# Who issues the loads of activations and gates in the value stage of a product-key expert layer

## Chip, cores and metric

The kernel runs on one core of one Trainium2 chip. The metric is the device time of one execution in microseconds, as the median of several runs. One more execution is taken under the hardware profiler, and every row of the trace below is from it.

## What is computed

One layer of a streaming encoder for 544 frames (512 of a prompt and 32 of a running stream) of width 1024, in float32: token mixers of two convolution groups, then a product-key retrieval over 128 x 128 experts with one neuron each, 8 heads with 16 experts per frame. Only the second half of the retrieval matters here:

```
act = gelu(einsum('td,thkd->thk', xt, u))      # u: the chosen experts' input rows
out = einsum('thk,thkd->td', gate * act, v)    # v: their output rows
```

For 384 of the 544 frames ("dense") the kernel doesn't gather. It multiplies them with all 16384 experts and lets a gate that is zero for the experts not chosen do the choosing. For the last 160 frames it gathers the chosen rows one slot at a time.

## The kernel before

The work goes through a stream of 300 units of weights, each 128 x 1024 float32 (512 KB): 20 of the input projection, 8 of the output projection, 16 of queries, 128 of u and 128 of v. A ring of four buffers (`raw`) takes them in. For near-float32 products, each unit is split in two: ScalarE copies it to `w_hi` (line 967), and GpSimd (line 504) or, from the value stage on, VectorE (line 1614) makes the rest `w_lo`. TensorE then runs three products for each chunk of 128 columns: hi x hi, hi x lo and lo x hi. A weight buffer is loaded again as soon as its unit is split (`load`, line 408, on the sync engine SP).

The u stage leaves the activations of each unit in DRAM (`acts_dram`, in pairs, line 1130) and the gates too (`gates_dram`, twelve groups of 32 frames, line 1175); both stores are issued by ScalarE. The value stage reads them back. A *quarter* is the activations of four units (768 KB, line 420) and goes to one of two buffers `acts_in`. A *group* is the gates of 16 units; it goes to `gates_even` or `gates_odd` in three pieces of 1 MB (line 426).

In the value stage VectorE's order for v = 0 to 127 is: the product of activations and gates of unit v + 4 (line 1651); one or two gathered rows added to the sums (line 1468); `w_lo` of unit v + 2 (line 1614); and `prod_lo` of unit v + 3 (line 1660). ScalarE's order is: `w_hi` of unit v + 2 (line 967), then `prod_hi` of unit v + 3 (line 1184), which waits for its product and until TensorE has finished unit v - 1, since `prod_hi` has four buffers. TensorE takes the units in order (line 912): 8 chunks, three products each. GpSimd fetches the gathered rows (line 568), up to eight ahead.

SP's order in this stage is written out in `value_group` (line 457). For each quarter it waits until the quarter's four products are made, issues the load of the quarter after next, then one piece of the next group's gates (quarters 0 to 2 of a group), then four loads of weights, each of which waits for the `w_lo` of the unit that had the buffer. So one queue carries weights, activations and gates. The loads of group 0's gates and of quarters 0 and 1 are issued ahead of the stage (lines 445 to 448).

Of the kernel before, what the change touches and what calls it, by code (L numbers as in the profile page):

```python
# [51 lines left out]
RING = 4  # L52
N_IN, N_OUT, N_Q = 5 * WC, KC, 2 * HEADS
N_U = NKEYS
N_V = NKEYS
GROUP = 16
GROUPS = N_V // GROUP
QUARTER = 4
QUARTERS = GROUP // QUARTER
GATE_PIECES = 3  # L60
# [20 lines left out]
GTS = DENSE // GT  # L81
# [17 lines left out]
AHEAD = 3  # L99
# [41 lines left out]
def build(nc, stream, x_t, params, sub_keys, u_rows, v_rows, final_g, y_t, y_rows, caches):  # L141
    gates_dram = nc.dram_tensor("gates_dram", (GTS, P, NKEYS, GT), F32, kind="Internal").ap()
    acts_dram = nc.dram_tensor("acts_dram", (N_U // 2, P, 2 * DENSE), F32, kind="Internal").ap()

    with ExitStack() as ctx:
        def sb_in(stack, name, shape, dt=F32):
            return stack.enter_context(nc.sbuf_tensor(name, shape, dt))
# [4 lines left out]
        def sem(name):  # L152
            return ctx.enter_context(nc.semaphore(name))
# [95 lines left out]
        acts_in = sb_in(values, "acts_in", [P, 2, QUARTER // 2, 2 * DENSE])  # L249
# [4 lines left out]
        gates_in = (gates_even, gates_odd)  # L254
# [56 lines left out]
        act_saved = [sem(f"act_saved{s}") for s in range(2)]  # L311
        acts_back = [sem(f"acts_back{s}") for s in range(2)]
        gates_back = [sem(f"gates_back{s}") for s in range(2)]
        prod_made = sem("prod_made")
# [63 lines left out]
        def wait_split(engine, lap, j, by_dve):  # L378

            if by_dve:  # L380
                engine.wait_ge(low_made, RING * (lap - LOW_LAP) + j + 1)
            else:
                engine.wait_ge(hi_made, RING * lap + j + 1)
                engine.wait_ge(lo_made, RING * lap + j + 1)
# [18 lines left out]

        @block.sync
        def _(sp):
            def load(lap, j, by_dve=False):

                if not (isinstance(lap, int) and lap == 0):  # L410
                    wait_split(sp, lap - 1, j, by_dve)
                src = stream[bass.ds(RING * lap + j, 1)].rearrange("a p n -> p (a n)")
                sp.dma_start(raw[:, j, :], src).then_inc(raw_in[j], 16)

            def load_acts(quarter, s):

                for n in range(2):
                    sp.wait_ge(act_saved[n], 16 * (quarter + 1))
                acts = acts_dram[bass.ds(2 * quarter, 2)].rearrange("e p t -> p e t")
                sp.dma_start(acts_in[:, s], acts).then_inc(acts_back[s], 16)  # L420

            def load_gates(group, s, piece):

                part = slice(piece * GTS // GATE_PIECES, (piece + 1) * GTS // GATE_PIECES)
                g = gates_dram[part, :, bass.ds(GROUP * group, GROUP), :].rearrange("g p e t -> p g (e t)")
                sp.dma_start(gates_in[s][:, part].rearrange("p g e t -> p g (e t)"), g).then_inc(gates_back[s], 16)

            def load_x(k):
                sp.dma_start(hid[:, k], x_t[:, k]).then_inc(x_in[k], 16)

            load_x(0)
            load(0, 0)
            for k in range(1, KC):
                load_x(k)
            for j in range(1, RING):
                load(0, j)
            first_load = FIRST_V // RING - U_AFTER + 2
            with sp.Fori(1, first_load) as lap:
                for j in range(RING):
                    load(lap, j)  # L440

            sp.wait_ge(g_saved[0], 16 * ((GTS + 1) // 2))
            sp.wait_ge(g_saved[1], 16 * (GTS // 2))
            first_value = FIRST_V // RING
            for piece in range(GATE_PIECES):
                load_gates(0, 0, piece)
            for s in range(2):
                load_acts(s, s)
            for lap in range(first_load, first_value + 1):
                for j in range(RING):  # L450
                    load(lap, j)
            for j in range(2):
                load(first_value + 1, j, True)
            sp.wait_ge(act_took, N_IN + N_Q + N_U)
            sp.dma_start(gain_rows[:], final_g).then_inc(gain_in, 16)

            def value_group(pair_lap, s, quarters=QUARTERS, gates_too=True):

                group = 2 * pair_lap + s
                for q in range(quarters):  # L460
                    sp.wait_ge(prod_made, GROUP * group + QUARTER * (q + 1))
                    load_acts(QUARTERS * group + q + 2, q % 2)
                    if q < GATE_PIECES and gates_too:
                        load_gates(group + 1, 1 - s, q)
                    for j in range(2, RING):
                        load(first_value + QUARTERS * group + q + 1, j, True)
                    for j in range(2):
                        load(first_value + QUARTERS * group + q + 2, j, True)

            with sp.Fori(0, GROUPS // 2 - 1) as pair_lap:  # L470
                value_group(pair_lap, 0)
                value_group(pair_lap, 1)
            value_group(GROUPS // 2 - 1, 0)
            value_group(GROUPS // 2 - 1, 1, QUARTERS - 2, gates_too=False)
            for j in range(2, RING):
                load(N_UNITS // RING - 1, j, True)
            sp.wait_ge(row_used, 2 * SLOTS)
            for g in range(PARTS):
                sp.dma_start(rows[0:PACKED, g, :], sums_x[g * PACKED:(g + 1) * PACKED, :]).then_inc(parts_in, 16)
            sp.wait_ge(y_rows_made, 1)  # L480
            sp.dma_start(y_rows[0:P], y_rows_sb[:]).then_inc(y_rows_saved, 16)
            sp.wait_ge(y_rows_made, 2)
            sp.dma_start(y_rows[P:GATHERED], rows[0:PACKED, PARTS, :]).then_inc(y_rows_saved, 16)
            sp.wait_ge(y_rows_saved, 32)
            sp.wait_ge(y_saved, 16 * 2 * len(Y_PIECES))
            sp.wait_ge(cache_saved, 16)
# [473 lines left out]
        def _(act):  # L960
            def split_high(lap, j):

                lap, j = lap + j // RING, j % RING
                act.wait_ge(raw_in[j], 16 * (lap + 1))
                if not (isinstance(lap, int) and lap == 0):
                    act.wait_ge(unit_done, RING * (lap - 1) + j + 1)
                nc.scalar.activation(w_hi[:, j, :], raw[:, j, :], ACT.Copy).then_inc(hi_made, 1)  # L967
# [49 lines left out]
            for u in range(N_IN):  # L1017
                c, part = (u - 2 * WC) // 3, (u - 2 * WC) % 3
# [161 lines left out]
            def product_high(v):  # L1180
                act.wait_ge(prod_made, v + 1)
                if v >= RING:
                    act.wait_ge(unit_done, FIRST_V + v - RING + 1)
                nc.scalar.activation(prod_hi[:, v % RING], prod[:, v % 2], ACT.Copy).then_inc(prod_hi_made, 1)  # L1184
# [18 lines left out]
            for v in range(N_V):  # L1203
                if v < N_V - 2:
                    split_high(FIRST_V // RING, v + 2)
                if v < N_V - AHEAD:
                    product_high(v + AHEAD)
                if v == 0:
                    act.wait_ge(row_used, SLOTS)
                    nc.scalar.activation(gelu[:], dots[:], ACT.Gelu).then_inc(gelu_made, 1)  # L1210
                if v == LAST_SUM + 2:
                    act.wait_ge(row_sum_made, 1)
                    nc.scalar.activation(row_std[:, 0:1], row_sum[:, 0:1], ACT.Sqrt, bias=eps[:],
                                         scale=1.0 / D).then_inc(row_std_made, 1)
                if v == LAST_SUM + 5:
                    act.wait_ge(row_sum_made, 2)
                    nc.scalar.activation(row_std[0:PACKED, 1:2], row_sum[0:PACKED, 1:2], ACT.Sqrt, bias=eps[0:PACKED],
                                         scale=1.0 / D).then_inc(row_std_made, 1)
# [602 lines left out]
```

## Time and profile before

| | us |
|---|---|
| runs shown | 1496.18, 1498.42, 1496.32 |
| median | 1496.32 |
| the profiled execution | 1497.36 |
| its span, from first to last instruction | 1495.5 |
| TensorE busy | 1444.0 |
| VectorE busy | 1249.6 |
| ScalarE busy | 630.6 |

The profiled execution is 1.86 us longer than its span, and 1.04 us above the median of the runs. The value stage lasts from about 937 us to the last matmuls near 1478 us. Busy times count instructions that compute; issuing a DMA and waiting don't count.

### The profile page before, as it was taken

What the parts mean: (1) busy time and instruction counts of PE and PEld (TensorE: products, weight loads), DVE (VectorE), ACT (ScalarE), POOL (GpSimd) and SP (SyncE); (2) the same over time, 40 slices, a digit from 0 to 9 for tenths busy, and PEclk for the clock granted to TensorE, in tenths of its full rate; (3) what the DMA queues carried; (4) which work ended last, traced back from release to release, by engine and by line L of the source; (5) the groups of instructions that cost most, each with busy time, mean ns of one, the idle gap of its engine ahead of it and who ended that gap; (6) DMA issues with size and microseconds to landing.
All of it is one profiled execution on the core that took longest, in us unless ns stands there. A gap on an engine that the chain in (4) does not pass through costs nothing.

```text
span 1495.5 us, 26608 instructions
## 1 busy us (share of the span) xinstructions
PE 1444.0 (97%) x9308; PEld 1423.0 (95%) x9308; DVE 1249.6 (84%) x2536; ACT 630.6 (42%) x848; POOL 886.8 (59%) x558
## 2 busy tenths in 40 slices
PE   7998989999999999999999997999999999999995
PEld 7998989999999999999999997999999999999984
DVE  7999874798999988688878841899999999999985
ACT  6234543333333333466666652333333333333331
POOL 4687434557688888666766675355555555555401
PEclk9999999999999999999999999999999999999997
DMA  4222213648699999789999999999999999999931
GB/s 179 97 77 69 98 59 120 218 171 296 211 339 330 323 344 335 257 325 352 379 359 364 367 370 329 388 378 396 386 409 380 410 386 375 407 380 414 357 115 46
DMA packets 125988, 433.37 MB, mean 290 GB/s; under 512 B 12480, under 2 KB 14784, under 8 KB 124256
## 3 DMA queue, kind: packets, MB, share of 16 engines
q1 hardware_dynamic: 66256, 211.57, 39.5%
q0 software_dynamic: 46080, 167.79, 29.6%
q10 hardware_dynamic: 13584, 53.25, 9.0%
q8 instruction: 24, 0.39, 0.1%
q14 instruction: 44, 0.36, 0.1%
HBM read 379.35 MB, written 52.69 MB: 289 GB/s over the span
## 4 chain that ended last, share of the span: by engine, by line
PE 81%; DVE 1%; DMA 1%; issue 0%; POOL 0%; ACT 0%; DVEq 0%; ACTq 0%
PE ps_unit L842 35%; PE ps_unit L912 18%; PE ps_misc L912 18%; PE ps_unit L817 6%; PE ps_misc L877 3%; DMA raw<-stream 1%; PE ps_misc L782 1%; PE ps_misc L786 0%; DVE y_sb L1760 0%; PE ps_unit L769 0%; DVE rows L1714 0%; DVE gate_parts L1603 0%; DVE gate L1556 0%; DVE rstd L1757 0%; POOL w_lo L504 0%
## 5 line engine op out<-in xcount | busy, mean ns | idle before, releaser
L504 POOL TENSOR_TENSOR w_lo<-raw,w_hi 128x1024 fp32r<-128x1024 f32 x172 | 415.8, 2419 | 215.4 <-issue 134.1
L568 POOL DMA_INDIRECT rows<-v_rows,expert x160 | 256.9, 1606 | 232.8 <-DVE sums L1468 159.9
L842 PE MATMUL ps_unit<-mov_hi,w_hi 128*128 128x384 f32 x1024 | 352.3, 344 | 8.6 <-POOL w_lo L504 8.6
L842 PE MATMUL ps_unit<-mov_lo,w_hi 128*128 128x384 f32 x1024 | 346.0, 338 | 0.0
L842 PE MATMUL ps_unit<-mov_hi,w_lo 128*128 128x384 f32 x1024 | 345.0, 337 | 0.0
L967 ACT ACTIVATE w_hi<-raw 128x1024 fp32r<-128x1024 f32 x300 | 315.2, 1051 | 60.2 <-ACT act_ring L1140 33.2
L1458 DVE CUSTOM_DVE_ANT_0 rows<-rows,ps_unit 128x1024 f32<-128x1024 f32 x160 | 190.4, 1215 | 30.1 <-DMA rows<-u_rows,expert 30.0
L1184 ACT ACTIVATE prod_hi<-prod 128x384 fp32r<-128x384 f32 x128 | 67.4, 526 | 320.8 <-PE ps_misc L912 320.4
L842 PEld LDWEIGHTS ps_unit<-mov_hi,w_hi 128*128 128x128 f32 x1024 | 193.1, 189 | 9.1 <-issue 9.1
L842 PEld LDWEIGHTS ps_unit<-mov_lo,w_hi 128*128 128x128 f32 x1024 | 193.3, 189 | 0.0
L842 PEld LDWEIGHTS ps_unit<-mov_hi,w_lo 128*128 128x128 f32 x1024 | 192.8, 188 | 0.0
L912 PE MATMUL ps_unit<-prod_hi,w_hi 128*128 128x384 f32 (+1 forms) x520 | 174.6, 336 | 6.2 <-DVE w_lo L1614 5.6
L912 PE MATMUL ps_unit<-prod_lo,w_hi 128*128 128x384 f32 (+1 forms) x520 | 174.1, 335 | 0.0
L912 PE MATMUL ps_unit<-prod_hi,w_lo 128*128 128x384 f32 (+1 forms) x520 | 173.9, 334 | 0.0
L568 POOL DMA_INDIRECT rows<-u_rows,expert x160 | 152.9, 955 | 33.8 <-issue 19.1
L1140 ACT ACTIVATE act_ring<-ps_unit 128x384 f32<-128x384 f32 x128 | 62.8, 491 | 257.1 <-PE ps_unit L842 257.1
L912 PE MATMUL ps_misc<-prod_hi,w_lo 128*128 128x384 f32 x508 | 169.9, 335 | 0.0
L912 PE MATMUL ps_misc<-prod_lo,w_hi 128*128 128x384 f32 x508 | 169.9, 334 | 0.0
L912 PE MATMUL ps_misc<-prod_hi,w_hi 128*128 128x384 f32 x508 | 169.8, 334 | 0.0
L1468 DVE SCALAR_TENSOR_TENSOR sums<-rows,weight,sums 128x1024 f32<-128x1024 f32 x128 | 163.8, 1280 | 3.6
L1614 DVE TENSOR_TENSOR w_lo<-raw,w_hi 128x1024 fp32r<-128x1024 f32 x128 | 155.9, 1219 | 4.2 <-issue 2.6
L1660 DVE TENSOR_TENSOR prod_lo<-prod,prod_hi 128x384 fp32r<-128x384 f32 x128 | 71.2, 556 | 47.6 <-ACT prod_hi L1184 46.5
(255 smaller groups left out, 2773.4 us busy)
## 6 DMA issues: line engine op xcount, KB each, us to landing
raw<-stream SPq DMA_DIRECT2D x300, 512.0 KB, 6.0
acts_dram<-act_ring ACTq DMA_DIRECT2D x64, 384.0 KB, 6.8
gates_dram<-gates ACTq DMA_DIRECT2D x12, 2048.0 KB, 10.8
acts_in<-acts_dram SPq DMA_DIRECT2D x32, 768.0 KB, 8.9
gates_even<-gates_dram SPq DMA_DIRECT2D x12, 1024.0 KB, 13.6
gates_odd<-gates_dram SPq DMA_DIRECT2D x12, 1024.0 KB, 12.9
rows<-u_rows,expert POOLq DMA_INDIRECT x160, 6.6
rows<-v_rows,expert POOLq DMA_INDIRECT x160, 8.1
```

The lines of the kernel that those rows point to most:

```text
L504: nc.gpsimd.tensor_tensor(w_lo[:, j, :], raw[:, j, :], w_hi[:, j, :].bitcast(F32), ALU.subtract).then_inc(lo_made, 1)
L568: nc.gpsimd.indirect_dma_start(out=rows[:, n % ROWS_RING, :], out_offset=None, in_=table, in_offset=bass.IndirectOffsetOnAxis(ap=expert[:, ...
L817: last = nc.tensor.matmul(ps_unit[:, a, 0:HALF], w[:, u % RING, k * P:(k + 1) * P], half(mov[:, k], a), start=(k == 0 and m == 0), stop=(k ...
L842: last = nc.tensor.matmul(dense_psum(j), w[:, j, k * P:(k + 1) * P], m[:, k, 0:DENSE], start=(k == 0 and n == 0), stop=(k == KC - 1 and n ...
L912: ins = nc.tensor.matmul(out, w[:, j, k * P:(k + 1) * P], m[:, j, part], start=(first and n == 0), stop=(last and n == 2))
L967: nc.scalar.activation(w_hi[:, j, :], raw[:, j, :], ACT.Copy).then_inc(hi_made, 1)
L1140: nc.scalar.activation(act_ring[:, j], dense_psum(j), ACT.Gelu).then_inc(act_took, 1)
L1184: nc.scalar.activation(prod_hi[:, v % RING], prod[:, v % 2], ACT.Copy).then_inc(prod_hi_made, 1)
L1458: nc.vector.tensor_tensor_reduce(out=rows[:, n % ROWS_RING, :], in0=rows[:, n % ROWS_RING, :], in1=x_rows, scale=1.0, scalar=0.0, op0=ALU. ...
L1468: nc.vector.scalar_tensor_tensor(out=total[:], in0=rows[:, n % ROWS_RING, :], scalar=weight[:, s:s + 1], in1=total[:], op0=ALU.mult, op1=A ...
L1614: nc.vector.tensor_tensor(w_lo[:, j, :], raw[:, j, :], w_hi[:, j, :].bitcast(F32), ALU.subtract).then_inc(low_made, 1)
L1660: nc.vector.tensor_tensor(prod_lo[:, v % RING], prod[:, v % 2], prod_hi[:, v % RING].bitcast(F32), ALU.subtract).then_inc(prod_lo_made, 1)
```

## The change

The two functions that load activations and gates take the issuing engine as an argument. SP still issues group 0's gates and quarters 0 and 1. All others are issued by ScalarE, in its loop over v: behind `prod_hi` of the last unit of a quarter (v + 3 = 3, 7, 11, ...) it issues the activations of the quarter after next and, for the first three quarters of a group, a piece of the next group's gates. SP's loop keeps four loads of weights per lap and has no wait for products.

```diff
+        def load_acts(engine, quarter, s):
+            for n in range(2):
+                engine.wait_ge(act_saved[n], 16 * (quarter + 1))
+            acts = acts_dram[bass.ds(2 * quarter, 2)].rearrange("e p t -> p e t")
+            engine.dma_start(acts_in[:, s], acts).then_inc(acts_back[s], 16)
+        def load_gates(engine, group, s, piece):
...
-                load_gates(0, 0, piece)
+                load_gates(sp, 0, 0, piece)
...
-                load_acts(s, s)
+                load_acts(sp, s, s)
...
-            def value_group(pair_lap, s, quarters=QUARTERS, gates_too=True):
-                group = 2 * pair_lap + s
-                for q in range(quarters):
-                    sp.wait_ge(prod_made, GROUP * group + QUARTER * (q + 1))
-                    load_acts(QUARTERS * group + q + 2, q % 2)
-                    if q < GATE_PIECES and gates_too:
-                        load_gates(group + 1, 1 - s, q)
-                    for j in range(2, RING):
-                        load(first_value + QUARTERS * group + q + 1, j, True)
-                    for j in range(2):
-                        load(first_value + QUARTERS * group + q + 2, j, True)
...
+            def value_lap(lap):
+                for j in range(2, RING):
+                    load(first_value + lap + 1, j, True)
+                for j in range(2):
+                    load(first_value + lap + 2, j, True)
+            with sp.Fori(0, N_V // RING - 2) as lap:
+                value_lap(lap)
...
                 if v < N_V - AHEAD:
                     product_high(v + AHEAD)
+                    quarter = (v + AHEAD) // QUARTER
+                    if (v + AHEAD) % QUARTER == QUARTER - 1 and quarter + 2 < N_V // QUARTER:
+                        load_acts(act, quarter + 2, quarter % 2)
+                        group, piece = quarter // QUARTERS, quarter % QUARTERS
+                        if piece < GATE_PIECES and group + 1 < GROUPS:
+                            load_gates(act, group + 1, (group + 1) % 2, piece)
```

## Rows read from the trace of the kernel before

**Rows 1.** Page, part 1: busy us (share of the span), instructions.

```profile
PE 1444.0 (97%) x9308; PEld 1423.0 (95%) x9308; DVE 1249.6 (84%) x2536; ACT 630.6 (42%) x848; POOL 886.8 (59%) x558
```

**Rows 2.** Stretches: length, busy of each engine, granted clock, DMA share, GB/s.

```profile
1045.00:1095.00 50.00, 50.00 (x290) 50.00 (x289) 46.12 (x53) 17.95 (x24) 25.67 (x17) 1.00 1.00 392
1145.00:1195.00 50.00, 50.00 (x290) 50.00 (x289) 46.70 (x53) 17.72 (x24) 27.03 (x17) 1.00 1.02 410
```

**Rows 3.** Chain that ended last, 945 to 1440 us, by line.

```profile
by line: PE ps_misc L912 50.1%; PE ps_unit L912 50.0%
```

**Rows 4.** Waits, 945 to 1440 us: total us, times, longest.

```profile
ACT prod_hi L1184 <- PE ps_misc L912: 309.8, 118, 3.0
...
DVE prod_lo L1660 <- ACT prod_hi L1184: 23.4, 35, 1.4
...
ACT w_hi L967 <- DMA raw<-stream: 8.8, 6, 2.5
```

**Rows 5.** Waits, 850 to 1490 us: those of PE.

```profile
PE ps_unit L842 <- POOL w_lo L504: 8.6, 1, 8.6
...
PE ps_unit L912 <- DVE w_lo L1614: 5.6, 1, 5.6
```

**Rows 6.** ScalarE in order of time, 700 to 730 us: start, length, instruction, idle before.

```profile
707.02 0.49 ACT L1140 ACTIVATE act_ring<-ps_unit 128x384 f32<-128x384 f32 x1 [1.73 <-PE ps_unit L842]
707.54 0.34 ACTq L1130 DMA_DIRECT2D acts_dram<-act_ring  x1
707.92 0.45 ACTq L1175 DMA_DIRECT2D gates_dram<-gates  x1
708.47 1.06 ACT L967 ACTIVATE w_hi<-raw 128x1024 fp32r<-128x1024 f32 x1 [0.96 <-ACT act_ring L1140]
...
718.40 1.06 ACT L967 ACTIVATE w_hi<-raw 128x1024 fp32r<-128x1024 f32 x1 [0.47 <-ACT act_ring L1140]
```

**Rows 7.** ScalarE in order of time, 1165 to 1200 us.

```profile
1170.32 0.53 ACT L1184 ACTIVATE prod_hi<-prod 128x384 fp32r<-128x384 f32 x1 [2.68 <-PE ps_misc L912]
...
1182.80 0.53 ACT L1184 ACTIVATE prod_hi<-prod 128x384 fp32r<-128x384 f32 x1 [2.68 <-PE ps_misc L912]
...
1195.28 0.53 ACT L1184 ACTIVATE prod_hi<-prod 128x384 fp32r<-128x384 f32 x1 [2.68 <-PE ps_misc L912]
```

**Rows 8.** Tile acts_in, SP, 883 to 900 us: issue ns min/median/max; us to landing.

```profile
L420 SPq DMA_DIRECT2D acts_in<-acts_dram x2: 3400/4208/5016, 888.5 to 893.6; - x2
...
DMA to landing us min/median/max: 19.3/20.9/22.4
```

**Rows 9.** SP's queue in order of time, 1150 to 1204 us.

```profile
1167.57 0.38 SPq L420 DMA_DIRECT2D acts_in<-acts_dram  x1
1168.14 0.38 SPq L426 DMA_DIRECT2D gates_even<-gates_dram  x1
```

**Rows 10.** VectorE in order of time, 1180 to 1200 us.

```profile
1183.36 0.56 DVE L1660 TENSOR_TENSOR prod_lo<-prod,prod_hi 128x384 fp32r<-128x384 f32 x1 [0.68 <-ACT prod_hi L1184]
1184.05 0.56 DVE L1651 TENSOR_TENSOR prod<-acts_in,gates_even 128x384 f32<-128x384 f32 x1
...
1187.11 1.22 DVE L1614 TENSOR_TENSOR w_lo<-raw,w_hi 128x1024 fp32r<-128x1024 f32 x1
```

**Rows 11.** Tile gates_even, SP, 945 to 1440 us.

```profile
DMA to landing us min/median/max: 12.2/13.2/15.6
```

**Rows 12.** Tile gates_even, SP, 883 to 890 us.

```profile
DMA to landing us min/median/max: 12.8/17.2/19.8
```

**Rows 13.** VectorE's groups, 945 to 1440 us: busy us, mean ns, idle before.

```profile
L1468 DVE SCALAR_TENSOR_TENSOR sums<-rows,weight,sums 128x1024 f32<-128x1024 f32 x128 | 163.8, 1280 | 3.6
...
L1468 DVE SCALAR_TENSOR_TENSOR sums_x<-rows,weight,sums_x 128x1024 f32<-128x1024 f32 x32 | 40.9, 1280 | 0.8
```

**Rows 14.** Tile acts_in, SP, 945 to 1440 us.

```profile
DMA to landing us min/median/max: 4.9/8.8/11.4
```

**Rows 15.** DMA queues, 945 to 1440 us: packets, MB, share of 16 engines.

```profile
q1 hardware_dynamic: 36394, 108.26, 56.3%
```

More of the change, by code:

```diff
@@ L401, in out_psum @@
             return sum_psum(q - 2) if q in (2, 3) else unit_psum(q)
+        def load_acts(engine, quarter, s):
[4 more added lines that the diff above has]
+        def load_gates(engine, group, s, piece):
+            part = slice(piece * GTS // GATE_PIECES, (piece + 1) * GTS // GATE_PIECES)
+            g = gates_dram[part, :, bass.ds(GROUP * group, GROUP), :].rearrange("g p e t -> p g (e t)")
+            engine.dma_start(gates_in[s][:, part].rearrange("p g e t -> p g (e t)"), g).then_inc(gates_back[s], 16)
         @block.sync
@@ L413, in load @@
                 sp.dma_start(raw[:, j, :], src).then_inc(raw_in[j], 16)
[L415 to L426, printed above, removed]
             def load_x(k):
@@ L455, in _ @@
             sp.dma_start(gain_rows[:], final_g).then_inc(gain_in, 16)
-            def value_group(pair_lap, s, quarters=QUARTERS, gates_too=True):
-                group = 2 * pair_lap + s
-                for q in range(quarters):
-                    sp.wait_ge(prod_made, GROUP * group + QUARTER * (q + 1))
-                    load_acts(QUARTERS * group + q + 2, q % 2)
-                    if q < GATE_PIECES and gates_too:
-                        load_gates(group + 1, 1 - s, q)
-                    for j in range(2, RING):
-                        load(first_value + QUARTERS * group + q + 1, j, True)
-                    for j in range(2):
-                        load(first_value + QUARTERS * group + q + 2, j, True)
[L470 to L474, printed above, removed]
+            def value_lap(lap):
[5 more added lines that the diff above has]
+                value_lap(lap)
             for j in range(2, RING):
```

## The prediction

> **What bounds the kernel now.** I read the page's first part, then the stretches of the value stage, then its chain and its waits, then single instructions around one group border. The page shows TensorE (PE) busy for 97% of the span, VectorE (DVE) for 84% and ScalarE (ACT) for 42% [rows 1]. The change touches only the value stage, so shares of the span settle nothing. In two stretches of that stage PE is busy 50.00 of 50.00 us at full granted clock, ACT about 18, DVE about 46.5, and the DMA share is at 1.0 while 392 to 410 GB/s move [rows 2]. The chain from 945 to 1440 us consists of PE's value matmuls and nothing else [rows 3]. The waits of that stretch name ACT (309.8 us waiting for PE before prod_hi), DVE (23.4 us waiting for ACT's prod_hi) and ACT once more (8.8 us for raw weights), but never PE [rows 4]. PE's waits lie at the stage's two ends: 8.6 us as the last u units starve, and 5.6 us near 1455 us, when DVE adds the packed rows before the last w_lo [rows 5]. So PE sets the time here, and anything the change does must reach PE to count.
>
> **The change part by part.** It moves 51 issues: the loads of quarters 2 to 31 (30 activation loads) and the gates of groups 1 to 7 in three pieces each (21). It takes SP's wait on prod_made out, and makes SP's loop one lap of four weight loads.
>
> *Weights no longer behind activations and gates: 0 us.* What earlier weights could shorten is a wait for raw. In this stretch only ACT has one, 8.8 us in six places [rows 4], on an engine with 309.8 us to spare, and DVE and PE never wait for w_hi there. The five loads that open the stage stay on SP, so the jam behind PE's 8.6 us stays [rows 5]. The 5.6 us stay too: they hang on DVE's order.
>
> *ACT's time for the issues: 0 us on the path.* ACT already issues such DMAs in the u stage: with one issue the gap to its next activation is 0.47 us, with two 0.96 [rows 6]. 21 pairs and 9 single ones make 21 x 0.96 + 9 x 0.47 = 24 us, beside 309.8 us idle. One at a time: an issue stands before the next w_hi, and ACT has 2.68 us free before each prod_hi [rows 7]. The new waits on act_saved are for spills long landed. What is queued behind the issue is w_hi, then prod_hi; DVE waits for them, and PE for DVE. The bad end is an issue that blocks: when five loads were issued in a row on SP, the activation issues took up to 5.0 us [rows 8]. That would make prod_hi 5.0 - 2.7 = 2.3 us late, under the cover worked out below. I take 0.96, since one pair at a time is the row that is alike.
>
> *The issue's place: this is where something gets late.* Near 1168 us SP issues the activations at 1167.57 and the gates at 1168.14 [rows 9]. The gates are the third piece of an even group. Their first reader is the DVE product at 1184.05, the first from gates_even, v = 64 [rows 10]. It follows, in order, the prod_lo of v = 62 at 1183.36, for which ACT's prod_hi started at 1182.80; three back, the prod_hi of v = 59 starts at 1170.32 [rows 7, 10]. Behind that one the change puts the issue. With the offsets of the u stage (first issue 0.52 us after the activation's start, second 0.38 later [rows 6]) the activations go out at 1170.84 and the gates at 1171.22: 3.1 us later than now. The gates may then take 1184.05 - 1171.22 = 12.8 us without anybody waiting.
>
> How long they will take on ACT's queue no row shows. The nearest row is the landing on SP's queue, 12.2 to 15.6 us with 13.2 in the middle [rows 11]; the far one is the pile of five loads at 884 us, 12.8 to 19.8 [rows 12]. I place it by what is left over. Weights need 524 kB per 4.16 us unit (three units from prod_hi at 1182.80 to that at 1195.28 [rows 7]), 126 GB/s. Gathered rows need 160 x 524 kB in 117 units, 172 GB/s (160 adds [rows 13], between FIRST_SUM 3 and LAST_SUM 120). Of 410 GB/s [rows 2] that leaves 112, and activations and gates of one quarter, 1.84 MB, take 16.4 us, the gates 16 from their own issue. I take 16 and keep 12.2 and 19.8 as ends. DVE then waits 16 - 12.8 = 3.2 us at a group border.
>
> For this one term a page speaks against the change. On one queue the trace shows 13.2 us in the middle [rows 11]. The Trainium skill (DMA: Bandwidth & Descriptors, section Queues, rings and completion order) says that each DMA engine goes round the queues that have work, one packet a turn. Here the code's runs are 4 KB for weights and rows, 3 KB for activations and 2 KB for gates. One run a packet is near what is counted, 36394 packets for 108.26 MB or 3.0 kB each on SP's queue [rows 15]. If all three queues are always full, activations get 3/11 and gates 2/10 of 410 GB/s, and both are in after 7.0 + 12.8 = 19.8 us, so that DVE would wait some 6.5 us; no run here shows it yet.
>
> *What hides DVE's wait.* In the iteration that starts with this product, DVE goes on to w_lo of v = 62, over at 1187.11 + 1.22 = 1188.33 [rows 10]. PE begins unit 62 when unit 61 is done, and that releases the prod_hi at 1195.28 [rows 7]: 6.95 us of cover. 3.2 us fit in it. DVE makes the delay good: its 23.4 us of waits for prod_hi [rows 4] over 495 / 4.16 = 119 units are 0.2 us a unit, 3 us a group. A DVE that runs late also needs the next gates later, so the wait doesn't add up from group to group. Activations alone are safe: 13.2 us from issue to the same product, against 11.4 at most [rows 14].
>
> *Sum.* 0 on PE from each part. The profiled execution took 1497.36 us for a span of 1495.5, 1.04 above the median of 1496.32; 0 added to that median is **1496.3 us**.
>
> **The rivals.** **Gates too late for PE (slower).** Place: the product that opens each of groups 1 to 7. From 12.8 + 6.95 = 19.8 us of landing on, the cover is gone and PE stops by what is beyond, each time anew, since PE's own delay moves ACT's issue as well. At 20.5 us that is 7 x 0.7 = 5 us (1501); at 22.4, the longest landing of the pile, the activations' [rows 8], 7 x 2.6 = 18 us (1514). For it speaks that the DMA engines are full [rows 2] and that 112 GB/s is only just over the 1.84 MB per 16.6 us quarter (110 GB/s) that the queue must carry. Against it: once DVE waits, weights and rows ask for less, and the gates get the rest. The packet turns of the page above would put the landing right at this point; the trace as it stands neither bears that out nor excludes it.
>
> **Earlier weights help after all (faster).** Its bound is PE's last wait, 5.6 us [rows 5], which would need an earlier last w_lo: 1490.7 at best. Against it: that w_lo stands behind DVE's row sums, not behind a transfer.
>
> **ACT's queue blocks at each pair.** At 5.0 us an issue [rows 8] DVE would get prod_hi 2.3 us late on top of 3.2 us for gates, 5.5 in all, still under 6.95: 1496.3. It only adds to the first rival's chance.
>
> **How the numbers follow.** A measurement of this kernel tells some 0.2% (3 us) from no change; the runs shown lie within 1496.18 to 1498.42. The forecast (PE never stops for it) gets 0.72, the late gates 0.23, the gain 0.04, the rest 0.01. A loss by late gates under 3 us would count as the same, one above as slower: 0.23 for slower, 0.04 for faster, 0.73 for the same. The range goes from 1493.8, the forecast less most of the 3 us, to 1504, which takes in the late gates up to about 1 us per group; the forecast's own range is 1494 to 1499.3.
>
> **What the changed profile would show.** Right: no wait of PE between 945 and 1440 us; acts_in and gates issues under ACTq about 3 us later than SP's; a new wait of DVE at line 1651 for gates, some seven times and 1 to 4 us each, with the 23.4 us of waits for prod_hi falling by about as much; raw landing sooner than before; ACT's gap before w_hi near 1 us every fourth unit. Wrong: PE waits for w_lo or prod_lo inside that stretch (the first rival), gates landing beyond 19.8 us, or activations that hold DVE in the middle of a group.

## The result, and the profile after

The changed kernel takes 1507.65 us (median of 4 runs, 1506.70 to 1511.19). The kernel before, run beside it, takes 1497.37 us (1496.18 to 1498.92). The ratio is 1.0071, with a 95% interval of 1.0054 to 1.0088: **slower by 0.7%**, some 10 us. The profiled execution took 1506.70 us for a span of 1504.9, so its span is 9.4 us longer than that of before.

The stretches of the value stage (columns as in [rows 2]) show where PE is no longer full:

```profile
1150.00:1184.00 34.00, 34.00 (x198) 34.00 (x197) 33.27 (x38) 13.14 (x17) 18.91 (x13) 1.00 1.03 414
...
1186.00:1197.00 11.00, 9.05 (x53) 8.73 (x51) 4.29 (x5) 3.06 (x4) 2.07 (x2) 1.00 0.69 278
1197.00:1204.00 7.00, 7.00 (x31) 7.00 (x32) 6.83 (x9) 2.42 (x4) 4.04 (x3) 0.76 0.90 291
```

Up to 1184 us all is as before: PE full, DMA engines full. In the eleven microseconds from 1186 us DVE is busy for 4.29 only and PE loses 2. Then PE is busy again, but with a granted clock of 0.76. The waits of 945 to 1450 us (total, times, longest) name what stood still:

```profile
ACT prod_hi L1175 <- DVE prod L1648: 36.7, 10, 5.2
ACT w_hi L958 <- DMA raw<-stream: 24.4, 24, 2.4
DVE prod L1648 <- DMA gates_odd<-gates_dram: 18.5, 4, 7.7
DVE prod L1648 <- DMA gates_even<-gates_dram: 18.3, 3, 7.9
...
ACT w_hi L958 <- issue: 8.4, 14, 0.8
...
DVE prod_lo L1657 <- ACT prod_hi L1175: 6.2, 9, 1.4
...
PE ps_unit L903 <- DVE w_lo L1611: 5.9, 5, 2.0
```

Against [rows 4], DVE has two new rows: it waits seven times for gates, once per group, 36.8 us in all. Its wait for prod_hi has shrunk from 23.4 to 6.2 us, and PE has a row where it had none: 5 waits for w_lo, 5.9 us. One border of groups, the same as in [rows 7, 9, 10], shows the chain in order. First ScalarE (start, length, instruction, idle before):

```profile
1170.12 0.53 ACT L1175 ACTIVATE prod_hi<-prod 128x384 fp32r<-128x384 f32 x1 [2.68 <-PE ps_misc L903]
1170.20 0.37 ACTq L411 DMA_DIRECT2D acts_in<-acts_dram  x1
1170.60 0.50 ACTq L417 DMA_DIRECT2D gates_even<-gates_dram  x1
1171.20 1.06 ACT L958 ACTIVATE w_hi<-raw 128x1024 fp32r<-128x1024 f32 x1 [0.55 <-issue]
```

Then VectorE:

```profile
1184.16 0.55 DVE L1657 TENSOR_TENSOR prod_lo<-prod,prod_hi 128x384 fp32r<-128x384 f32 x1
1192.60 0.56 DVE L1648 TENSOR_TENSOR prod<-acts_in,gates_even 128x384 f32<-128x384 f32 x1 [7.89 <-DMA gates_even<-gates_dram]
...
1195.66 1.22 DVE L1611 TENSOR_TENSOR w_lo<-raw,w_hi 128x1024 fp32r<-128x1024 f32 x1
```

And the chain of waits over 1150 to 1210 us (start, length, what), which before held nothing but PE [rows 3]:

```profile
1170.60 21.93 DMA gates_even<-gates_dram
...
1192.60 0.06 DVE prod L1648
...
1195.66 1.23 DVE w_lo L1611
...
1196.94 3.81 PE ps_unit L903 x12
1200.74 2.21 PE ps_misc L903 x12
```

The gates are issued at 1170.60, 2.5 us later than before, and land at 1192.5 instead of 1180.3. DVE needed them at about 1184.7, stands for 7.89 us, makes w_lo at 1195.66 instead of 1187.11, and PE, which wanted it at 1195.0, begins at 1196.94. Its first twelve matmuls then take 3.81 us instead of 2.08.

Over the stage, the landing of gates by tile (gates_even, then gates_odd, 945 to 1440 us) answers to [rows 11]:

```profile
DMA to landing us min/median/max: 16.9/20.2/21.9
...
DMA to landing us min/median/max: 12.0/18.7/22.3
```

From a median of 13.2 us the landing of gates_even has gone to 20.2. Weights land in 7.3 us (median) as before; activations went from 8.8 to 9.1, gathered rows from 8.1 to 9.4.

Of the 9.4 us in the span, 5.9 are PE's waits, and 1.9 the slow matmuls behind the first of them (3.81 + 2.21 instead of 2 x 2.08). Behind three of the four other stops the first twelve matmuls take 2.35 to 2.37 us at a granted clock of 1.00, 0.8 us more together than at 2.08. The rest, under 1 us, is not accounted for.

### The profile page after: what moved, and what is told of

Read it like the earlier page. It is cut to its first block, busy times and chain, and to the rows that moved or that the text cites. A ratio compares the mean times of both kernels' runs of the same rounds, so it can differ in the third digit from the quotient of the medians.

```text
span 1504.9 us, 26602 instructions
## 1 busy us (share of the span) xinstructions
PE 1446.2 (96%) x9308; PEld 1423.3 (95%) x9308; DVE 1244.6 (83%) x2536; ACT 635.7 (42%) x848; POOL 888.0 (59%) x558
## 4 chain that ended last, share of the span: by engine, by line
PE 74%; DMA 7%; DVE 2%; issue 1%; ACT 0%; POOL 0%; ACTq 0%; DVEq 0%
PE ps_unit L833 35%; PE ps_unit L903 15%; PE ps_misc L903 14%; PE ps_unit L808 6%; PE ps_misc L868 3%; DMA gates_odd<-gates_dram 3%; DMA gates_even<-gates_dram 3%; DMA raw<-stream 1%; PE ps_misc L773 1%; DVE w_lo L1611 0%; DVE sums L1465 0%; PE ps_misc L777 0%; DVE y_sb L1757 0%; PE ps_unit L760 0%; DVE rows L1711 0%
## 5 line engine op out<-in xcount | busy, mean ns | idle before, releaser
L903 PE MATMUL ps_unit<-prod_hi,w_hi 128*128 128x384 f32 (+1 forms) x520 | 175.9, 338 | 12.1 <-DVE w_lo L1611 11.5
L903 PEld LDWEIGHTS ps_unit<-prod_hi,w_hi 128*128 128x128 f32 x520 | 98.9, 190 | 14.3 <-DVE w_lo L1611 13.4
## 6 DMA issues: line engine op xcount, KB each, us to landing
gates_even<-gates_dram ACTq DMA_DIRECT2D x9, 1024.0 KB, 20.2
```

The lines of the kernel that those rows point to most:

```text
L903: ins = nc.tensor.matmul(out, w[:, j, k * P:(k + 1) * P], m[:, j, part], start=(first and n == 0), stop=(last and n == 2))
```

## Experiments

The theory is **sharing**: the gates land late because activations and gates, on a queue of their own, get only that queue's turns at the DMA engines. The rivals are **place** (the issue is 2.5 to 3 us later, and that alone does it) and **ScalarE's own work** (51 more issues on it). All ratios are against the kernel before, run on the same chip.

**1. Late issue, old queue.** The kernel before, with SP held back to where ScalarE issues:

```diff
-                    sp.wait_ge(prod_made, GROUP * group + QUARTER * (q + 1))
+                    sp.wait_ge(prod_hi_made, GROUP * group + QUARTER * (q + 1))
```

> The kernel before, with one edit: SP waits for the prod_hi of a quarter's last unit instead of its products, so that it issues activations and gates where ScalarE does after the change, some 3 us later, but still on the one queue with the weights. Theory (sharing: a queue of its own gets only a share of the DMA engines' turns): the third gates still land in 12 to 15.6 us, DVE waits at most 3 us at a group border, PE never stops between 945 and 1440 us, and the time is that of the kernel before within 0.2%. Rival (place: the 3 us later issue alone does it): DVE waits 5 to 8 us at the borders, PE stops in the stage, and the time is near 1507 us.

Measured: 1497.02 us, ratio 0.9997 (0.9987 to 1.0006). The landing of gates_even, then DVE's one wait for it:

```profile
DMA to landing us min/median/max: 10.0/11.0/14.3
...
DVE prod L1651 <- DMA gates_even<-gates_dram: 2.2, 1, 2.2
```

The gates even land a little sooner than the 12 to 15.6 us expected, and PE never waits between 945 and 1440 us. On the old queue, place alone costs nothing.

**2. Early issue, new queue.** The changed kernel, ScalarE issuing one unit sooner:

```diff
-                    if (v + AHEAD) % QUARTER == QUARTER - 1 and quarter + 2 < N_V // QUARTER:
+                    early = (v + AHEAD) % QUARTER == QUARTER - 2
+                    if (early or v == 0) and quarter + 2 < N_V // QUARTER:
+                        act.wait_ge(prod_made, QUARTER * (quarter + 1))
                         load_acts(act, quarter + 2, quarter % 2)
```

> The changed kernel, with ScalarE's issues one unit (4.16 us) earlier, behind the prod_hi of the last unit but one of a quarter and a wait for the quarter's last product; only the first quarter's stays. Three queues as after the change. Sharing: the third gates still take 19 to 22 us to land, DVE's wait at a border falls from up to 7.9 us to at most 4, which is under the cover of 6.95 us, so PE doesn't stop and the time is back within 0.2% of before. Place alone: gates land in about 13 us and DVE waits nowhere. Rival (ScalarE's own work: the issues delay w_hi and prod_hi): as many issues, so the loss of some 10 us stays.

Measured: 1498.46 us, ratio 1.0003 (0.9994 to 1.0013). Gates_even and gates_odd land thus, and PE is full from 945 to 1395 us:

```profile
DMA to landing us min/median/max: 13.2/15.5/20.7
...
DMA to landing us min/median/max: 15.1/17.9/20.8
...
945.00:1395.00 450.00, 450.00 (x2598) 450.00 (x2597) 416.12 (x470) 163.25 (x218) 239.49 (x146) 1.00 1.00 391
```

The transfers are still slow, if less so than expected (third gates 13 to 20 us, not 19 to 22), but no longer late: DVE's longest wait for gates is 2.8 us. ScalarE has as many issues as after the change, so its own work is out.

**3 and 4. One of the two kinds of load back on SP.**

Both restore SP's `value_group` with its wait for products. In run 3 SP issues the gates there, and ScalarE's `load_gates` goes:

```diff
+                    sp.wait_ge(prod_made, GROUP * group + QUARTER * (q + 1))
+                    if q < GATE_PIECES and gates_too:
+                        load_gates(sp, group + 1, 1 - s, q)
...
-                            load_gates(act, group + 1, (group + 1) % 2, piece)
```

> The changed kernel with the gates back on SP at their place of before (SP's loop written out); ScalarE issues only the activations. Sharing: the gates have the weights' queue and nothing of the activations ahead of them, so they land in about 12 us or less, DVE doesn't wait for gates, PE doesn't stop, and the time is within 0.2% of before; the activations land in 8 to 12 us, in time. Rival (any third queue slows all of them): gates over 16 us, DVE waits, PE stops, time over 1502 us.

In run 4 it is the other way round:

```diff
+                    sp.wait_ge(prod_made, GROUP * group + QUARTER * (q + 1))
+                    load_acts(sp, QUARTERS * group + q + 2, q % 2)
...
-                        load_acts(act, quarter + 2, quarter % 2)
```

> The changed kernel with the activations back on SP at their place of before; ScalarE issues only the gates, 3 us later than before. Sharing, with the queue's length as the reason: 1 MB alone on ScalarE's queue lands in 10 to 15 us, DVE waits at most 2 us at a border, PE doesn't stop, time within 0.2% of before. If the gates' 2 KB runs against 4 KB ones set their share, whatever lies ahead: 1.05 MB at 82 GB/s, 13 to 16 us, DVE waits up to 3 us, PE still doesn't stop. Rival (place alone): DVE waits as after the change and the time stays near 1507 us.

Measured: with the gates on SP 1497.65 us, ratio 1.0000 (0.9990 to 1.0009); with the activations on SP 1497.49, ratio 0.9997 (0.9988 to 1.0007). In the first the gates land in 12.6 us (median, 15.2 at most), a little above the 12 expected, and DVE never waits for them. In the second the gates are alone on ScalarE's queue and land thus (gates_odd), while DVE waits for them five times, 11.5 us in all, and PE never:

```profile
DMA to landing us min/median/max: 12.9/15.4/17.5
```

That is nearer the second of the two expectations, in which the 2 KB runs set the gates' share whatever lies ahead of them; DVE's longest wait, 4.0 us, is beyond its 3. So the loss needs both loads on the one new queue, the gates behind the activations. Place alone is out a second time: here the gates are issued as late as after the change.

**5. The dose raised.** The changed kernel, issuing one unit later:

```diff
-                    quarter = (v + AHEAD) // QUARTER
-                    if (v + AHEAD) % QUARTER == QUARTER - 1 and quarter + 2 < N_V // QUARTER:
+                    quarter = (v + AHEAD) // QUARTER - 1
+                    if v > 0 and (v + AHEAD) % QUARTER == 0 and quarter + 2 < N_V // QUARTER:
```

> The changed kernel, with ScalarE's issues one unit (4.16 us) later, the dose raised. The gates may now take 12.8 - 4.2 = 8.7 us before DVE waits and 8.7 + 6.95 = 15.6 before PE stops. Sharing with a deadline: at landings of 19 to 21 us PE stops 3 to 5 us at each of seven borders, 21 to 35 us in all, so 1518 to 1533 us. Rival (the loss is what ScalarE spends on issues, or the third queue slows transfers everywhere): as many issues and queues as after the change, so the time stays near 1507 us.

Measured: 1533.0 us, ratio 1.0231 (1.0214 to 1.0248). The waits from 945 to 1480 us, and two stretches around one border:

```profile
DVE prod L1648 <- DMA gates_odd<-gates_dram: 34.3, 4, 9.8
DVE prod L1648 <- DMA gates_even<-gates_dram: 29.7, 3, 10.5
...
PE ps_unit L903 <- DVE w_lo L1611: 22.3, 6, 4.8
```

```profile
1120.00:1137.00 17.00, 14.35 (x83) 14.03 (x81) 7.27 (x9) 3.67 (x6) 5.05 (x4) 1.00 0.78 311
1137.00:1150.00 13.00, 11.37 (x56) 11.37 (x57) 12.79 (x15) 4.93 (x7) 7.31 (x5) 0.87 0.83 295
```

PE stops at six of the seven borders (at the first the gates land in 14.8 us), 3.7 us each, within the 3 to 5 expected. The median is at the upper end of the forecast, because the waits are not the whole price: behind this stop the granted clock is 0.87 over 13 us. Behind each of the six, 24 matmuls take 6.0 to 7.1 us instead of 4.16, some 13 us in all, and with the 22.3 us of waits that makes up the loss of 34.9.

**6. The weights' runs halved: told nothing.**

```diff
...
+                if by_dve:
+                    src = src.rearrange("a p (h n) -> p (a h) n", h=2)
+                    sp.dma_start(raw[:, j, :].rearrange("p (h n) -> p h n", h=2), src).then_inc(raw_in[j], 16)
...
```

> The changed kernel, with each value weight load asked for in runs of 2 KB where it had 4 KB; same bytes, same places. If the DMA engines take turns packet by packet and a run is a packet, weights now get 2 KB per turn, the gates' share rises from 2/10 to 2/8, and activations and gates are in after about 16 us: the third gates land in 15 to 18 us, PE stops little or not at all, the time falls to 1497 to 1502 us, and raw takes longer to land than 7.3 us. Rival (shares go by bytes, or by what each queue asks): gates still land in 19 to 22 us, time near 1507 us.

Measured: 1505.24 us, ratio 1.0047 (1.0031 to 1.0064). The weights' queue (packets, MB, share), after the change and in this run:

```profile
q1 hardware_dynamic: 16760, 60.99, 31.4%
```

```profile
q1 hardware_dynamic: 16856, 61.38, 31.7%
```

Half-size runs would have added 128 packets to each of 116 loads. They didn't: the bytes per packet are the same, and the run is in effect a repeat of the changed kernel.

**7. The gates' runs doubled.** The changed kernel with another layout of the gates in DRAM, so that a load finds 4 KB in one piece:

```diff
-    gates_dram = nc.dram_tensor("gates_dram", (GTS, P, NKEYS, GT), F32, kind="Internal").ap()
+    gates_dram = nc.dram_tensor("gates_dram", (GTS // 2, P, GROUPS, 2, GROUP * GT), F32, kind="Internal").ap()
...
+            g = gates_dram[part.start // 2:part.stop // 2, :, group].rearrange("g p b n -> p g (b n)")
+            dst = gates_in[s][:, part].rearrange("p (g b) e t -> p g (b e t)", b=2)
...
+                act.dma_start(gates_dram[tg // 2, :, :, tg % 2, :],
+                              gates[:, s].rearrange("p (g e) t -> p g (e t)", e=GROUP)).then_inc(g_saved[s], 16)
```

> The changed kernel with the gates laid out in DRAM so that each run of a gate load is 4 KB where it was 2 KB (the u stage stores them in 2 KB runs); same bytes, same issues, same places. The run before it on this question (weights in 2 KB runs) changed no packets: the queue of the weights shows 16856 packets for 61.4 MB as after the change, so it told nothing. If the DMA engines take turns packet by packet, gates now get 4/12 instead of 2/10 of the turns' bytes while all queues are full: 137 instead of 82 GB/s, the third gates land in 13 to 16 us instead of 19 to 22, DVE waits at most 4 us, PE doesn't stop in the value stage, the time is back at 1496 to 1499 us. Rival (shares go by bytes or by demand, not by packets): gates still land in 19 to 22 us, PE stops, time near 1506 us.

Measured: 1498.46 us, ratio 1.0007 (0.9997 to 1.0016). ScalarE's queue, after the change and in this run:

```profile
q10 hardware_dynamic: 19095, 45.15, 23.8%
```

```profile
q10 hardware_dynamic: 13604, 44.80, 23.2%
...
DMA to landing us min/median/max: 10.8/16.7/17.5
...
DMA to landing us min/median/max: 10.7/16.3/16.7
```

This time the packets are fewer for the same bytes, 3.3 kB each instead of 2.4. Gates_even and gates_odd land in 16.7 and 16.3 us instead of 20.2 and 18.7, though issued at the same places. Third gates take 11.6 to 17.5 us (13 to 16 were expected), DVE waits 14.1 us in all and 4.5 at most, PE not at all. With the same bytes in fewer packets the loss is gone, as sharing by packets has it.

**8 and 9. The opening loads moved, and the tail mended.** PE's waits at the two ends [rows 5] are much the same after the change (8.1 and 5.6 us), so both kernels can be beaten there. Run 8 moves the five opening loads from SP to ScalarE, one per u unit; run 9 also moves DVE's adding of the packed rows behind the last w_lo.

```diff
...
+                    if at in (0, 2, 3):
+                        load_gates(act, 0, 0, (0, 2, 3).index(at))
+                    if at in (1, 4):
+                        load_acts(act, (1, 4).index(at), (1, 4).index(at))
...
-                if v == LAST_SUM + 4:
+                if v == LAST_SUM + 5:
```

> The kernel before (all steady loads on SP), with the five opening loads (group 0's gates, quarters 0 and 1) moved to ScalarE, one per u unit from the third unit after the gate groups on, so that the last u weights don't queue behind 4.7 MB. Theory (queueing behind a bulk in one queue is what PE's 8.6 us wait and ScalarE's 12.8 us wait for raw are): both waits go, the time falls by 6 to 11 us to 1487 to 1492. Rival (the DMA engines are full there whoever issues, or the loads come too late for the first products): PE waits elsewhere near 915 to 940 us, time within 0.2% of before.

> As the run with the opening loads on ScalarE, and DVE adds the packed rows one unit later, behind the last w_lo. Theory (PE's 5.6 us wait near 1455 us hangs on DVE's order alone): that wait goes, and the time falls by a further 4 to 7 us, to 1481 to 1488. Rival (the last sums of DVE run late for it): PE's wait goes but the end after the last matmul grows by as much.

Measured: 1495.43 us, ratio 0.9983 (0.9974 to 0.9993), a miss (1487 to 1492 were expected); and 1488.44, ratio 0.9940 (0.9923 to 0.9956), for both, just above the 1481 to 1488 expected. The waits of run 8, at 850 to 945 us:

```profile
ACT act_ring L1134 <- DMA acts_dram<-act_ring: 5.4, 1, 5.4
...
PE ps_unit L836 <- POOL w_lo L498: 4.7, 1, 4.7
```

The weights are no longer behind the bulk, but now ScalarE's stores of activations are: they stand in its queue behind the opening loads, ScalarE waits 5.4 us for one, splits the next weights late, and PE still stops for 4.7 us. In run 9 the wait near 1455 us falls from 5.6 to 1.4 us.

**10 and 11. The opening loads stay on SP, spread.** Run 10 is the kernel before with the tail's edit, and SP issues one opening load behind each of five weights. Run 11 makes the same two edits in experiment 2's kernel, where ScalarE issues early.

```diff
...
-            for piece in range(GATE_PIECES):
-                load_gates(0, 0, piece)
-            for s in range(2):
-                load_acts(s, s)
+            opening = [lambda p=p: load_gates(0, 0, p) for p in range(GATE_PIECES)]
+            opening += [lambda s=s: load_acts(s, s) for s in range(2)]
             for lap in range(first_load, first_value + 1):
                 for j in range(RING):
                     load(lap, j)
...
+                    if opening:
+                        opening.pop(0)()
```

> The kernel before with two edits away from the change: SP issues the five opening loads one at a time between the last u weights and the first value weights, and DVE adds the packed rows one unit later. Theory (the opening loads hurt because weights queue behind 4.7 MB at once; behind 1 MB they land in time): PE's waits near 915 us shrink from 8.6 to under 4 us, its wait near 1455 us to under 2, and the time falls to 1484 to 1489 us, a little under the run with the opening loads on ScalarE. Rival (the first products then come too late): DVE waits for gates beyond 925 us and PE stops before the first value units, time over 1490 us.

> The same two edits on the changed kernel with ScalarE's issues one unit earlier. If who issues the steady loads is worth nothing once they are in time, the time is that of the run beside it within 0.2%. Rival (weights on a queue of their own help once the ends are mended): over 0.2% faster than the run beside it.

Measured: 1483.35 us, ratio 0.9909 (0.9892 to 0.9926), a little below the range expected; and 1483.66, ratio 0.9910 (0.9894 to 0.9927). PE's waits in run 10, 850 to 1490 us:

```profile
PE ps_unit L843 <- POOL w_lo L505: 1.5, 1, 1.5
...
PE ps_unit L913 <- DVE w_lo L1615: 1.4, 1, 1.4
```

8.6 and 5.6 us have become 1.5 and 1.4. This is the fastest version here, and it does without the change. With the change mended, the time is the same.

## Why the prediction was wrong

**The bound** was read rightly: PE sets the time, and the loss is what reached PE.

**Weights no longer behind activations and gates: 0 us.** Right for the time. The sign I gave for it was wrong: raw lands in 7.3 us in the median as before, and ScalarE waits longer for it, 24.4 us instead of 8.8.

**ScalarE's time for issues: 0 us.** Right. Experiment 2 has all 51 issues and no loss. The view of waits shows 8.4 us of them before w_hi, less than the 24 of the sum.

**The issue's place: 3.1 us later.** Nearly right: 2.5 us, because ScalarE issues 0.08 us after the activation's start and doesn't wait for its end, as it did in the u stage, where the store needs the result. Experiment 1 shows that this part alone costs nothing.

**The landing on ScalarE's queue: this step failed.** I took 16 us, from the bandwidth that weights and rows leave over on average, 112 GB/s, and from a queue that is empty when the load is issued. The third gates took 19.2 to 22.3 us at six of seven borders. Both parts of the step were wrong, and the border at 1170 us shows by how much. First, the queue was not empty. The gates issued one quarter earlier, at 1153.96 us, landed thus:

```profile
DMA to landing us min/median/max: 19.8/19.8/19.8
```

That is at 1173.8 us, 3.6 us after the next activations were issued. From there to 1192.5 the quarter's 1.84 MB took 18.7 us, 98 GB/s, more than the 16.6 us that a quarter lasts. So most quarters with gates leave a rest to the next one, until the fourth, which has activations only. My rival named this margin (110 GB/s needed of 112), but the 16 us made nothing of it.

Second, the rate. The left-over rate supposes that the other queues ask for their mean and no more. But weights and rows are asked for as fast as buffers come free, and while they have packets waiting, the new queue gets its turns and no more. From 1182 to 1190 us, while the third gates cross, the queues of gathered rows (q0), weights (q1) and gates (q10) move (packets, MB, share):

```profile
q0 software_dynamic: 368, 1.32, 40.7%
q1 hardware_dynamic: 351, 1.31, 40.4%
q10 hardware_dynamic: 339, 0.68, 22.1%
```

The packets are nearly the same in number, the bytes are not: gates get 85 GB/s, weights 164 where I had reckoned with 126. I also held against the rival that weights and rows ask for less once DVE waits. DVE stands from 1184.7 us on, but the DMA engines stay full until the gates are nearly in (columns as in [rows 2]):

```profile
1185.00:1192.00 7.00, 7.00 (x42) 7.00 (x41) 0.00 (x0) 1.59 (x2) 0.06 (x1) 1.00 1.03 413
```

The far end of my range, 19.8, was the nearer one. On the rate, row and rule had pulled apart, and the rule was the better guide: the Trainium skill (DMA: Bandwidth & Descriptors, Queues, rings and completion order) has each DMA engine go round its queues packet by packet. The trace agrees, with the three counts above. By that rule the prediction had 19.8 us from the first issue to the last byte, from an empty queue; the trace has 18.7 us, and 3.6 ahead of it for the rest of the quarter before. With 4 KB runs for the gates an estimate by the rule is 7.0 + 7.7 = 14.7 us; the third gates land after 11.6 to 17.5, on both sides of it.

**The cover, 6.95 us, and the point 19.8 us** from which PE stops: the point held up, its two parts did not. DVE began to wait 13.7 to 15.9 us after the issue, not 12.8, and at the four borders where PE stopped, 4.1 to 5.9 us of DVE's wait stayed hidden from it, not 6.95. At the border shown the parts are 14.1 + 5.9 = 20.0, so that two errors cancelled, which is luck. With landings of 14.5, 19.3 and 19.2 us at the first three borders PE doesn't stop; with 21.9, 22.0, 20.7 and 22.3 at the other four it stops for 1.95, 2.05, 0.69 and 1.23 us (the last in two stops, 0.89 and 0.34). Price per border as the first rival had it (landing less 19.8) is 2.1, 2.2, 0.9 and 2.5.

**The rivals and the chances.** What happened is the first rival, whose price was put at 5 to 18 us and is 10, though PE stopped at four borders and not at seven. It got 0.23 and a range that ended at 1504. With a landing that no row showed, a cover that ended just at the upper bound, and full DMA engines, 16 us deserved no such weight against 19.8. What the price left out is the clock: 1.9 us behind the first stop, on top of the wait itself. So the 10 us are in part another sum than the rival's.

## What to carry to other kernels

Where the DMA engines are full, moving loads to a second queue doesn't add bandwidth: it changes who gets the turns, and the loads with the shortest runs lose. Before moving one, take its deadline from the trace (first reader less issue) and compare it with a landing at that queue's share of turns, not at the rate the others leave over on average. And a bulk of loads issued at once hurts whatever stands behind it in the same queue, weights on SP or stores on ScalarE; spread between the small loads, PE's wait there fell from 8.6 to 1.5 us.

The Trainium skill says of this (DMA: Bandwidth & Descriptors, Issuing engines are not separate DMA queues) that issuing from several engines only saves the sequencer's time. That the steady loads gain nothing else from it agrees with runs 10 and 11 (1483.35 and 1483.66 us). The section names no cost; here there was one (ratio 1.0071).

## What was not expected of the hardware

A stop of PE for 1.95 us was followed by matmuls at nearly half their rate: twelve in 3.81 us instead of 2.08, with a mean granted clock of 0.76 from 1197 to 1204 us, which is a stretch at the lower of the two levels (1.2 GHz) and the rest at 2.4. Ahead of the stop PE had been busy without a gap at 1.00. Not every stop did this: the next one, 2.05 us near 1267 us, has a granted clock of 1.00 around it, and so have the shorter ones. In experiment 5 all six stops, of 2.8 to 4.8 us, did: the stretches of 6 to 10 us around their ends have mean granted clocks of 0.62 to 0.76. Why the 1.95 us stop did and the 2.05 us one did not, these runs don't show.

An access written as two halves of a contiguous row gave packets of the same mean size as the whole row, 3.6 kB (experiment 6), so the number of packets has to be read from the trace before a run on transfer shapes is believed.
